# A recurrent scan whose turns run in three stages abreast, with two buffers for what crosses them

## What is computed

```python
sa = jnp.einsum('bhvk,bhk->bhv', S, kk_t)
S = (S * w_t[:, :, None, :] - sa[..., None] * (kk_t * a_t)[:, :, None, :]
     + v_t[..., None] * k_t[:, :, None, :])
return S, jnp.einsum('bhvk,bhk->bhv', S, r_t)
```

## Time and profile before

| | us |
|---|---|
| median of 3 runs | 4312.69 (4312.33 to 4316.23) |
| profiled execution | 4314.55 |
| its span | 4312.8 |
| granted TensorE clock, mean of the span | 0.946 of full |
| first to last instruction of `rwkv_scan` | 2401.88 to 2741.68 |

### The profile page before, as it was taken

One profiled execution on the slowest core, in us unless ns is written; L12 is line 12 of the kernel. 1 busy time (PEld: TensorE's weight loads), 2 busy tenths in 40 slices (PEclk: granted clock), 3 DMA queues, 4 the chain that ended last, 5 costly groups with the idle time before them and its releaser, 6 DMA issues. The chain is left out here.

```text
span 4312.8 us, 67312 instructions
## 1 busy us (share of the span) xinstructions
PE 3819.4 (89%) x27854; PEld 3112.8 (72%) x27854; DVE 2118.5 (49%) x3453; ACT 1416.6 (33%) x2565; POOL 32.1 (1%) x52
## 2 busy tenths in 40 slices
PE   7989999998889999969888588789999899668998
PEld 5767777767767777758666477678888788567887
DVE  5575644434765644441554655543332426574334
ACT  3333532223334422231443233332222223363222
POOL 0000000000000000000000000000000000000000
PEclk8999999999999999979999799999999999789999
DMA  5341444433333444411011000111221120002332
GB/s 156 88 103 52 152 143 147 166 106 99 97 79 94 143 149 163 160 45 45 1 49 39 3 4 4 48 49 59 64 64 58 49 79 30 1 20 79 97 97 78
DMA packets 312373, 340.85 MB, mean 79 GB/s; under 512 B 23680, under 2 KB 289696, under 8 KB 305568
## 3 DMA queue, kind: packets, MB, share of 16 engines
q1 hardware_dynamic: 311424, 332.59, 24.1%
q10 hardware_dynamic: 672, 4.36, 0.4%
HBM read 316.48 MB, written 20.45 MB: 78 GB/s over the span
## 5 line engine op out<-in xcount | busy, mean ns | idle before, releaser
L274 DVE TENSOR_TENSOR weights_lo<-weight_ring,weights_hi 128x1024 fp32r<-128x1024 f32 x371 | 454.4, 1225 | 1375.1 <-ACT weights_hi L270 1375.1
L270 ACT ACTIVATE weights_hi<-weight_ring 128x1024 fp32r<-128x1024 f32 x371 | 392.8, 1059 | 1605.1 <-PE banks L321 1533.9
L321 PE MATMUL banks<-mlp_x_lo,weights_hi 128*128 128x512 f32 (+1 forms) x1280 | 479.8, 375 | 0.0
L321 PE MATMUL banks<-mlp_hidden_hi,weights_hi 128*128 128x512 f32 (+1 forms) x1280 | 476.9, 373 | 0.0
L321 PE MATMUL banks<-mlp_hidden_lo,weights_hi 128*128 128x512 f32 (+1 forms) x1280 | 476.3, 372 | 0.0
L321 PE MATMUL banks<-mlp_hidden_hi,weights_lo 128*128 128x512 f32 (+1 forms) x1280 | 475.7, 372 | 0.0
L321 PE MATMUL banks<-normed_hi,weights_hi 128*128 128x512 f32 (+1 forms) x1040 | 360.8, 347 | 21.8 <-ACT normed_hi L288 19.7
L321 PE MATMUL banks<-mlp_x_hi,weights_hi 128*128 128x512 f32 x768 | 307.4, 400 | 20.9 <-DVE mlp_x_lo L305 9.5
L321 PE MATMUL banks<-mlp_x_hi,weights_lo 128*128 128x512 f32 x768 | 304.9, 397 | 0.0
L321 PEld LDWEIGHTS banks<-mlp_hidden_hi,weights_hi 128*128 128x128 f32 x1280 | 241.1, 188 | 51.6 <-issue 6.7
L321 PEld LDWEIGHTS banks<-mlp_x_lo,weights_hi 128*128 128x128 f32 x1280 | 242.8, 190 | 44.7
(11 more groups left out here) (552 smaller groups left out, 6994.9 us busy)
## 6 DMA issues: line engine op xcount, KB each, us to landing
weight_ring<-in_w SPq DMA_DIRECT2D x64, 1024.0 KB, 5.3
mod_chunks<-in_mod_w SPq DMA_DIRECT2D x24, 2048.0 KB, 9.8
weight_ring<-in_w_in SPq DMA_DIRECT2D x42, 1024.0 KB, 5.4
weight_ring<-in_w_up SPq DMA_DIRECT2D x32, 1024.0 KB, 5.6
weight_ring<-in_w_down SPq DMA_DIRECT2D x32, 1024.0 KB, 5.1
weight_ring<-in_w_in SPq DMA_DIRECT2D x52, 512.0 KB, 4.3
weight_ring<-in_w_out SPq DMA_DIRECT2D x16, 1024.0 KB, 5.2
gate_logits_dram<-gates_staged SPq DMA_DIRECT2D x48, 256.0 KB, 4.5
```

Of the source, the lines that this page charges most:

```text
L270: act.activation(self.w_hi[:, t % 2], self._raw(t), ACT.Copy).then_inc(self.w_rounded, 1)
L274: dve.tensor_tensor(self.w_lo[:, t % 2], self._raw(t), self.w_hi[:, t % 2].bitcast(F32), ALU.subtract)\
L321: mm = pe.matmul(bank, a[:, k, :], b[:, k, t0:t0 + w], start=(k == 0 and n == 0), stop=(k == KD - 1 and n == 2))
```

## The change

The list `order` is written anew, and a pass over it is now a period i instead of a turn. In period i a direction runs the levels of chunk i, the front of chunk i+1 (`there(i + 1)`) and the tail of chunk i-1 (`there(i - 1)`); there are 14 periods, from -1 to 12. What must outlive its period has two buffers, taken by the chunk's parity (`scored`, `kr`, `kb_tok`, `v_tok`), or three (`ends`). The last level's result has a buffer of its own (`solution`), and `grow` no longer lies in `zx`. The results of `cross` go to `t.a` and `t.b` instead of `t.c` and `t.d`. Moved are also: v's turn (from `turn` into the pairs of apply 3, with an ACT step `v` of its own), the growth of g (from apply 2 into apply 1, followed by the product of `kr` with the state), `g` (from DVE to ACT), the state's growth (apply 3 to apply 2), the output's growth (apply 4 into one group with `solve`), `out` (behind apply 3) and the read of the state (from behind grow_by 5 into one group with the product for the state, the step `push`). The five bending products stay on DVE. For room, six rows of `x` (`x2`) are set aside too, and a buffer `rw_extra` of 1024 columns is new.

```diff
-    order = [("pe", "apply", 1, 0), ("dve", "keep", 1, 0), ("pe", "turn", 0, 0), ("pe", "grow_by", 1, 0),
...
+    order = [("pe", "apply", 1), ("dve", "keep", 1), ("act", "g", 0), ("pe", "grow_by", 1), ("act", "merge", 1),
...
     def run(engine, step):
-        own = [(on, name, l, turn + ahead) for turn in range(-1, turns) for on, name, l, ahead in order]
+        own = [(on, name, l, period) for period in range(-1, turns + 1) for on, name, l in order]
...
+            def apply(t, l, i):
+                level, tail, front = there(i), there(i - 1), there(i + 1)
...
+                if level and l == 1:
+                    pe.wait_ge(t.started, i + 1)
+                    pe.wait_ge(t.masked, i + 1)
+                if level and l > 1:
+                    pe.wait_ge(t.merged[l - 1], i + 1)
+                if tail and l == 1:
+                    pe.wait_ge(t.token_major, i)
+                    pe.wait_ge(t.v_copied, i)
+                    pe.wait_ge(t.merged[5], i)
+                if tail and l == 2:
+                    pe.wait_ge(t.g_copied, i)
+                    done(i, t.token_major)
...
+                for q, h, half, other in heads():
+                    if level:
+                        mm = one(t.d[half, 1, q, :], scored[other, h, q, 0:64], x[other, q, :])
...
+                    if tail and l == 1:
+                        one(t.c[half, 1, q, :], old_scored[half, h, q, 0:64], t.v_tok[old][half, q, :], start=q == 0)
+                    if tail and l == 2:
+                        one(t.a[half, 0, q, :], t.kb_tok[old][half, h, q, :], t.v_tok[old][half, q, :], start=q == 0)
+                    if front and l == 3:
...
+                        mm = one(t.c[half, 1, q, :], f[half, RW_V + q, at:at + 64], same[half, :])
...
+                if tail and l == 1:
...
+                    for q, h, half, _ in heads():
+                        mm = one(t.c[half, 1, q, :], t.kr[old][half, q, 0:64], t.state[half, q, :], start=False)
+                    mm.then_inc(t.gathered, 1)
+                if tail and l == 2:
+                    for q, h, half, other in heads():
+                        mm = one(t.c[other, 1, q, :], t.solution[half, q, :], t.g0[half, q, :])
...
+                        one(t.b[half, 0, q, :], t.v_tok[old][half, q, :], old_scored[half, h, q, 64:P], start=q == 0)
+                if tail and l == 3:
+                    pe.wait_ge(t.state_made, i)
+                    for q, h, half, other in heads():
+                        mm = one(t.b[half, 0, q, :], t.u[other, q, :], old_scored[other, h, q, 64:P], start=False)
...
+                elif name == "push" and there(i - 1):
+                    old = (i - 1) % 2
+                    pe.wait_ge(t.u_copied, i)
+                    for q, h, half, other in heads():
+                        one(t.b[half, 0, q, :], t.state[half, q, :], t.kr[old][half, q, 64:P], start=False)
+                        mm = one(t.a[half, 0, q, :], t.kb_tok[old][other, h, q, :], t.u[other, q, :], start=False)
...
+                elif name == "join" and there(i + 1):
+                    kr = t.kr[(i + 1) % 2]
+                    pe.wait_ge(t.rest_bent, i + 2)
+                    pe.wait_ge(t.started, i + 2)
...
+                aside = [y[:, c, :] for c in range(4)] + [x2[:, c, :] for c in range(6)]
```

More of the change, by code:

```diff
@@ L2543, in rwkv_scan @@
         pass
-    rooms, used = (kit.ring, spare), [0, 0]
+    rooms = [kit.ring, *spare]
+    used = [0] * len(rooms)
     def take(*dims):
         n = 64 * math.prod(dims)
-        r = 0 if used[0] + n <= RING_FLOATS else 1
+        r = next(r for r in range(len(rooms)) if used[r] + n <= rooms[r].shape[-1])
         used[r] += n
@@ L2597, in rwkv_scan @@
[L2597 to L2601, removed]
+    order = [("pe", "apply", 1), ("dve", "keep", 1), ("act", "g", 0), ("pe", "grow_by", 1), ("act", "merge", 1),
+             ("pe", "apply", 2), ("dve", "keep", 2), ("act", "u", 0), ("act", "grow", 0), ("dve", "bend", 0),
+             ("pe", "grow_by", 2), ("act", "merge", 2), ("pe", "push", 0), ("dve", "state", 0), ("dve", "bend_rest", 0),
+             ("pe", "apply", 3), ("dve", "keep", 3), ("act", "v", 0), ("act", "y", 0),
+             ("pe", "grow_by", 3), ("act", "merge", 3), ("pe", "cross", 0), ("dve", "start", 0),
+             ("pe", "apply", 4), ("dve", "keep", 4), ("pe", "grow_by", 4), ("act", "merge", 4),
+             ("pe", "join", 0), ("dve", "mask", 0),
+             ("pe", "apply", 5), ("dve", "keep", 5), ("pe", "grow_by", 5), ("act", "merge", 5),
+             ("pe", "turn", 0), ("act", "token_major", 0)]
@@ L2635, in apply, with grow_by @@
+            def grow_by(t, l, i):
                 if l == 1:
[L2636 to L2639, removed]
+                    done(i - 1, t.g_copied)
                 if l == 2:
[L2641 to L2661, removed]
-                    mm = one(t.c[half, 0, q, :], t.yl[l][half, q, :], z[half, q, :])
-                    if l < 5:
-                        mm = one(t.d[other, 0, q, :], z[half, q, :], t.yl[l][half, q, :])
-                mm.then_inc(t.grown_by[l], 1)
-                if l == 5:
-                    for q, h, half, other in heads():
-                        mm = one(t.b[half, 1, q, :], t.state[half, q, :], t.kr[half, q, 64:P], start=False)
-                    mm.then_inc(t.read, 1)
@@ new lines, in grow_by @@
+                if l == 3:
+                    done(i + 1, t.v_copied)
+                if there(i):
+                    z = t.first[:, 0] if l == 1 else t.zx[:, 0]
+                    pe.wait_ge(t.kept[l], i + 1)
+                    for q, h, half, other in heads():
+                        mm = one(t.c[half, 0, q, :], t.yl[l][half, q, :], z[half, q, :])
+                        if l < 5:
+                            mm = one(t.d[other, 0, q, :], z[half, q, :], t.yl[l][half, q, :])
+                    mm.then_inc(t.grown_by[l], 1)
```

259 lines of the change are left out of this document (135 added, 124 removed).

## The result

The changed kernel takes 4284.66 us (median of 4 runs, 4281.64 to 4288.32), the kernel before 4314.46 on the same chip (4312.33 to 4317.06): ratio 0.9928, 95% interval 0.9914 to 0.9942. It is 30 us faster; forecast were 51.3 less, 4261.4, and the time lies above the range's end (4281). The profiled execution took 4283.83, its span is 4282.0.

A forecast was written before the change was run, and what follows sets the result against it. No engine was full, so a chain of waits was taken to bound the recurrent scan. Scan 13.1 + 2.4 + 267.5 + 5.5 = 288.5 against 339.8, 51.3 us less: 4263.2 profiled, 4261.4 as median; range 4250 to 4281.

The forecast's parts named there:

- (1) The work: Scan: products per direction and chunk stay 208, work per period almost unchanged, but 14 instead of 12 periods are walked.
- (2) PE's time, 17.5 per period: TensorE in the scan: 15 groups of 0.47, a join and a turn make 8.7 us per direction, 17.5 per period.
- (3) The period, 22.2: Scan, one chunk in both directions: 21.9 us from hops plus 0.3 for semaphores gives 22.2, against 26.64 before.
- the walk of 21.6: Scan: hop prices summed along the written order, always from the last instruction; 10.81 us per half period, 21.6 per period.
- The 1.2% on top: Scan period: the same walk of the kernel before gave 26.3 against 26.64 measured, so 1.2% was added, giving 21.9.
- the extra semaphores: New groups in the scan carry more semaphores: at most 0.09 us each, half taken, 0.3 per period.
- (4) Ends: Scan's start and end: 13.1 us before the levels, 2.4 for the slow clock, 5.5 for the last chunk's tail.
- (5) The set-aside is hidden: rwkv_prepare and rwkv_finish: moving six more rows, 7.7 us each way, is covered; without cover both ways cost 15.
- dear hops: Rival, chance 0.14: each of 34 hops per scan period comes 0.04 later; period 23.5, 15.7 us more, 4277.
- the masks over 23 apart: Scan: sign that the forecast is wrong through hops; masks of one direction were forecast 21.6 to 22.8 us apart.
- Paired products take turns: Rival, chance 0.03: four newly paired TensorE groups per direction cost 0.47 each after all; period 26.0, 46 us more, 4307.
- round trips: Rival, chance 0.05: g, u, v, push wait on PE products, three 1.2 us trips per half period; period 28.8, 4341.

The follow-up runs named there:

- train 3: Kernel before plus, behind its scan, a hardware loop of 16 turns around four groups of 32 independent records; the train took 34 us, 15.8 ns per record.
- train 1: Kernel before plus, behind its scan, 64 groups of 32 independent records written out, 4096 instructions without waits; the train took 57 us.
- a_few: Changed kernel without three of TensorE's growths, 192 fewer instructions per period, output not the reference's; 4261.54 us, ratio 0.9883.
- b_few: Kernel before without three of TensorE's growths, 192 fewer instructions per period, output not the reference's; 4304.77 us, ratio 0.9979.
- a_more: Changed kernel with 16 unread products per direction and chunk added on idle quarters, 128 more instructions per period; 4318.03 us, ratio 1.0009.
- b_more: Kernel before with 48 unread products per direction and chunk added on idle quarters, 384 more instructions per period; 4367.33 us, ratio 1.0124.
- a_order: Changed kernel with only the written order of its steps changed, all 1713 instructions per period kept; 4293.02 us, ratio 0.9947 to the kernel before.

## Why the prediction was wrong

Its direction and mechanism were right: the tail and the front left the chain, and the scan shrank. Point by point, on the profiled execution (forecast 4263.2, measured 4283.83, 20.6 more):

- **(1) The work**: right, 9984 and 192 records. It counted products and never asked what it takes to bring their instructions.
- **(2) PE's time, 17.5 per period, "no bound below 17.5"**: the step that failed. 32 records do take 0.5 (the rows around 2571 have them 0.016 apart), and train 3 confirms it over 1873 records. But TensorE wasn't given 1713 new instructions in that time: at 3.5 us per block they need 6.7 x 3.5 = 23.4 us, at the 3.67 of train 1 they need 24.6. The bound was 23.4 to 24.6, not 17.5, and the prediction had no term for it. The hint was there: the queue named "instruction" had a packet every 4.0 us before, 3.3 at the least, and the change asks for 6.7 in 22.2 us, one per 3.3, so the shortest distance ever seen would have had to be the average.
- **(3) The period, 22.2**: 24.7, so 12.05 x 2.5 = 29.6 us too short. Without most of the stalls it is 22.5 (a_few), and 0.8 per period of that are stands still, so the walk of 21.6 and its hops were about right. The 1.2% on top, from 21.6 to 21.9, were probably not overhead of hops but the same stall, small, in the kernel before (b_few: 26.3). Whether the extra semaphores cost 0.3 was not measured alone.
- **(4) Ends, 21.0 beside the 12.05 periods**: 313.8 - 12.05 x 24.66 = 16.7, 4.3 less than forecast. The first forward masks are only 18.0 apart, since that period has no tail yet. The slow clock at the scan's start lasted 21 us in both kernels (a mean of 0.50 over the 21.2 us until 2420.1; before, 0.62 over the 28.1 us until 2430.0); what it cost in each was not measured apart from the missing tail.
- **(5) The set-aside is hidden**: right. Windows of both phases in the changed kernel:

```profile
2355.00:2365.00 10.00, 3.77 (x14) 1.98 (x12) 5.97 (x6) 9.81 (x18) 0.00 (x0) 0.85 0.00 0
2371.00:2398.00 27.00, 0.00 (x0) 0.00 (x0) 26.20 (x31) 0.00 (x0) 0.00 (x0) 0.50 0.00 0
2713.00:2728.00 15.00, 12.38 (x33) 6.73 (x33) 14.56 (x27) 2.58 (x4) 0.00 (x0) 0.89 0.97 330
2741.00:2750.00 9.00, 9.00 (x52) 6.67 (x50) 8.79 (x15) 0.00 (x0) 0.00 (x0) 1.00 0.00 0
```

  All rows are out by 2355 and back by 2741, under VectorE's 26.2 of 27 us as before. 3.0 us were gained ahead of the scan and 1.8 behind it; of the 3.0, 2.7 had built up by 550 us already, in code that is the same, so they are of the runs.
- **The rivals**: *dear hops* gave 4277 by the wrong cause and was nearest in time; the masks over 23 apart, which the prediction called its sign, had a cause that no case named. *Paired products take turns* did not come. The sign set for *round trips* did, ScalarE waiting for PE before u over 1 us each time, but it was badly chosen. ScalarE's waits before u between 2450 and 2655 (in total, times, longest), of the changed kernel and of a_few:

```profile
ACT rw_extra L2780 <- PE banks L2630: 17.6, 8, 3.1
ACT x L2780 <- PE banks L2630: 17.0, 8, 2.6
```

```profile
ACT x L2775 <- PE banks L2630: 12.4, 9, 1.7
ACT rw_extra L2775 <- PE banks L2630: 12.4, 9, 1.7
```

  They are 2.2 us each and 1.4 each. 1.4 stay in a kernel whose period is 22.5, near the walk's, so they seem to lie beside the chain; the other 0.8 are probably TensorE's stands passed on. The range was too narrow because it priced everything that an engine does, and not its supply.

The sum: 29.6 - 4.3 - 3.0 - 1.8 = 20.5 of the 20.6.

## What to carry to other kernels

Straight-line code with many small matmuls has a second ceiling beside the array's: count instructions, two to a record, and compare the blocks of 256 with the packets of the instruction queue in the profile. Here a run of blocks that could be done in under 3.5 us each stalls as soon as the one block kept ahead is used up, however slow the stretch ahead of it was, so filling idle quarters with more small products no longer comes free. The cure is then fewer instructions for the same sums (taller products), and only after that a better order.

## Not expected of the hardware

- A block of 256 instructions of TensorE that is brought anew takes about 3.5 us or more: 3.47 to 4.02 from one resumption to the next in train 1, packets 3.27 to 3.49 apart at the least in every kernel, and only one block is kept ahead (205 records after a lull, then 128 by 128). A loop of 256 instructions is not brought again (one packet in 29 us).
- The pace differs between chips or runs: packets on average 3.70 apart between 2450 and 2655 in the changed kernel's first profile, 3.86 in its second, and the ratio to before went from 0.9928 to 0.9954. What sets it stays open.
- The granted clock can dip inside the scan: in the second profile of the changed kernel, windows of 30 us show 0.94 (at 2450 and at 2480, with matmul records over 25.9 and 24.4 of the 30 us), as do windows of a_more and b_more. In the first profile it is 1.00 from 2420 to the scan's end, and in a_order, whose packets come 3.81 us apart, it is 1.00 in the eight such windows from 2420 to 2660. So whether the stands bring the dips about isn't shown. They may be part of why a_more and b_more lie above the walk; how large a part was not measured.
- Records on four quarters can start 15.8 ns apart on average over 1873 records (train 3).
